# Issuing the loads of five meta weight groups one weight unit sooner in the sync engine's list

## What is computed

```python
h = jnp.concatenate([filler, meta, x], axis=1)
u = rms_norm_2(h, pre_mix_gain[l])
proj = u @ w_in[l]
qa, ka, va, qb, kb, vb, g = jnp.split(proj, SPLITS, axis=-1)
...
k_meta = k[:, META_PAD:BLOCK]
v_meta = v[:, META_PAD:BLOCK]
```

## Time and profile before

| | |
|---|---|
| median of 3 runs | 842.55 us |
| the profiled execution, its own time | 842.99 us |
| its span | 841.1 us |
| TensorE busy with matmuls | 804.5 us (96%) |
| VectorE busy | 498.6 us (59%) |
| ScalarE busy | 468.4 us (56%) |
| mean granted clock of TensorE | 0.989 |
| loads of meta_w: issue to landing, median | 8.4 us |

### The profile page before, as it was taken

How to read it: one execution, slowest core, us unless ns; L and a number is a source line. 1 busy time by engine, 2 the same in 40 slices (tenths; PEclk the granted TensorE clock), 3 DMA queues, 4 the chain that set the end, 5 groups by cost and what they waited for, 6 DMA issues and landing times.

```text
span 841.1 us, 12690 instructions
## 1 busy us (share of the span) xinstructions
PE 804.5 (96%) x4238; PEld 651.6 (77%) x4238; DVE 498.6 (59%) x731; ACT 468.4 (56%) x1004; POOL 137.4 (16%) x204
## 2 busy tenths in 40 slices
PE   7999999999999995979999999999999999999996
PEld 5877877886777884767778888878887888888884
DVE  5456565584665555656666667666686644555454
ACT  5677585575666464436665656454656533444352
POOL 2011021000342110343335354100000000000000
PEclk9999999999999998899999999999999999999999
DMA  8974552468764546343233444556675646465631
GB/s 241 275 186 141 145 170 101 151 201 253 223 201 132 203 130 198 102 133 91 61 87 102 115 132 134 165 159 219 230 237 179 206 126 198 152 198 189 211 128 51
DMA packets 147294, 137.78 MB, mean 164 GB/s; under 512 B 15024, under 2 KB 115648, under 8 KB 147232
## 3 DMA queue, kind: packets, MB, share of 16 engines
q1 hardware_dynamic: 145136, 129.89, 50.2%
q0 software_dynamic: 2096, 7.09, 3.0%
HBM read 135.90 MB, written 1.05 MB: 163 GB/s over the span
## 4 chain that ended last, share of the span: by engine, by line
PE 80%; DMA 4%; POOL 4%; ACT 4%; DVE 3%; issue 2%; SPq 1%; DVEq 0%; ACTq 0%; POOLq 0%
PE psum L1176 64%; PE psum L1154 6%; DMA meta_w<-in_w_in 4%; PE psum L1275 3%; PE psum L1410 3%; PE psum L1196 1%; ACT w_hi L1457 1%; POOL rtmp L1122 1%; PE psum L1378 1%; POOL rtmp L1124 1%; DVE w_lo L1653 1%; POOL rtmp L1126 1%; POOL stage L1128 1%; DMA raw<-in_w_in 1%; ACT probs L1584 1%
## 5 line engine op out<-in xcount | busy, mean ns | idle before, releaser
L1653 DVE TENSOR_TENSOR w_lo<-raw,w_hi 128x1024 fp32r<-128x1024 f32 (+1 forms) x234 | 273.9, 1193 | 121.6 <-ACT w_hi L1457 85.8
L1176 PE MATMUL psum<-w_hi,h_hi 128*128 128x512 f32 (+1 forms) x656 | 259.3, 395 | 5.0 <-DVE h_lo L1711 4.1
L1457 ACT ACTIVATE w_hi<-raw 128x1024 fp32r<-128x1024 f32 (+1 forms) x234 | 230.8, 1011 | 44.2 <-PE psum L1176 18.6
L1176 PE MATMUL psum<-w_lo,h_hi 128*128 128x512 f32 (+1 forms) x656 | 246.8, 376 | 0.0
L1176 PE MATMUL psum<-w_hi,h_lo 128*128 128x512 f32 (+1 forms) x656 | 246.3, 375 | 0.0
L1176 PEld LDWEIGHTS psum<-w_hi,h_hi 128*128 128x128 f32 x656 | 124.0, 189 | 31.6 <-issue 15.0
L1176 PEld LDWEIGHTS psum<-w_lo,h_hi 128*128 128x128 f32 x656 | 123.7, 189 | 19.2
L1176 PEld LDWEIGHTS psum<-w_hi,h_lo 128*128 128x128 f32 x656 | 124.1, 189 | 15.3
L1176 PE MATMUL psum<-w_hi,m_hi 128*128 128x512 f32 x152 | 60.3, 397 | 1.6 <-DVE m_lo L1711 1.5
L1176 PE MATMUL psum<-w_lo,m_hi 128*128 128x512 f32 x152 | 59.3, 390 | 0.0
L1176 PE MATMUL psum<-w_hi,m_lo 128*128 128x512 f32 x152 | 59.2, 389 | 0.0
(11 more groups left out here) (171 smaller groups left out, 1006.0 us busy)
## 6 DMA issues: line engine op xcount, KB each, us to landing
raw<-in_w_in SPq DMA_DIRECT2D x112, 256.0 KB, 3.6
raw<-in_w_ffn_in SPq DMA_DIRECT2D x88, 256.0 KB, 4.0
raw<-in_w_in SPq DMA_DIRECT2D x24, 512.0 KB, 3.9
raw<-in_w_out SPq DMA_DIRECT2D x24, 512.0 KB, 3.5
raw<-in_w_in SPq DMA_DIRECT2D x64, 192.0 KB, 2.7
raw<-in_w_ffn_out SPq DMA_DIRECT2D x22, 512.0 KB, 4.4
meta_w<-in_w_in SPq DMA_DIRECT2D x10, 1024.0 KB, 8.4
raw<-in_w_mem_kv SPq DMA_DIRECT2D x8, 512.0 KB, 3.6
```

Of the source, the lines that this page charges most:

```text
L1176: last = nc.tensor.matmul(psum[:, bank, 0:n], sx[name][:, c, t * P:(t + 1) * P], wx[:, kk, 0:n], start=u["first"] and kk == 0 and z == 0, ...
L1457: nc.scalar.activation(weights(u)[0][:, :, 0:n], raw[:, u["raw"], :, 0:n], ACT.Copy)\
L1653: nc.vector.tensor_tensor(lo[:, :, 0:n], raw[:, u["raw"], :, 0:n], hi[:, :, 0:n].bitcast(F32), ALU.subtract)\
```

## The change

```diff
--- before.py
+++ after.py
@@ -716,7 +716,8 @@
     units = [arg for what, arg in line if what in ("unit", "unit_a") or (what == "flush" and arg and "chunks" in arg)]
     for g in metas:
         at = line.index(("meta", g) if g["n"] != 3 else ("flush", dict(g=g)))
-        after = sum(any(arg is u for u in units) for what, arg in line[:at] if what != "unit_b")
+        after = sum(what in ("unit", "unit_a") or (what == "flush" and arg is not None and "chunks" in arg)
+                    for what, arg in line[:at])
         units[after + META_LOAD[g["n"]]]["then_meta"] = g
     pl.steps = lay_out(line)
     number(pl, pl.steps)
```

## The result

The changed kernel takes 834.39 us (median of 4 runs, 833.52 to 835.22); the kernel before, run beside it, 842.28 us (840.41 to 844.26). The ratio is 0.9906, with a 95% interval of 0.988 to 0.9932: faster by 0.9%, 7.9 us. The forecast was 835.2, with a range of 832.6 to 838.6.

What follows compares the result with a forecast made beforehand. TensorE, busy 804.5 of 841.1 us, bounds the kernel, so only its waits and clock can give. Terms 1.1 + 5.6 + 0.6 = 7.3 us, from 842.55 to 835.2 us; range 832.6 to 838.6.

Steps and rivals of the forecast that it cites:

- Groups 0 and 2: TensorE's waits for the meta weights ahead of these groups go: 0.9 and 0.2 us, together 1.1 us.
- The pair leaves at once after group 3's matmuls: Group 4's two load DMAs wait only for group 3's matmuls and leave at 322.05 us, 5.0 us sooner.
- Its landing: Group 4's pair takes 8.7 us and lands at 330.75 instead of 336.37 us, a gain of 5.6 us.
- The clock: At group 4 the clock still falls in the idle time, costing 1.7 instead of 2.3 us: 0.6 us back.
- The norm as the next bound: At full clock, normed tile 0 sets the start of the transposes behind group 4, allowing at most 7.4 us.
- (a): Rival: ring order alone, no traffic ahead of group 4's pair; load gain 6.9 us, total 8.6, 833.9 us; chance 0.24.
- (b): Rival: the clock doesn't fall in group 4's 3 us wait; gains 8.8 us, 833.8 us; chance 0.12.
- signs that the forecast is wrong: Pair over 10 us, growing `xn` or `h_lo` wait, 0.50 clock beyond 4.6 us, or new `w_hi` or `w_lo` waits.
- signs that it is right: `meta_w` wait about 3.0 us, pair leaving at once, landing 8 to 9 us later, no new `raw` wait, TensorE less busy.
- (c): Rival: the unit behind slows group 4's pair to 10.9 us; gains 5.1 us, 837.4 us; chance 0.09.
- (d): Rival: gain handed back by another wait, further clock falls or a load leaving no sooner; 841 us or so; chance 0.05.
- (e): Rival: moved units land late and hold ScalarE's split, 20 us lost less 7.3 won; 855 us; chance 0.03.

Runs made afterwards that it cites:

- groups 0 to 3 alone: Kernel before, with only the load pairs of groups 0 to 3 issued one unit sooner; 840.56 us, ratio 0.9984.
- two units sooner: Changed kernel, with group 4's pair of loads issued one more unit sooner; 834.71 us, ratio 0.9918.
- filled kernel before: Kernel before, with 18 extra TensorE matmuls, never read, in the wait ahead of group 4; 839.73 us, ratio 0.9969.
- norm ahead of splits: Changed kernel, with the splits of two weight units moved behind the first norm at the border of the blocks; 836.23 us, ratio 0.9933.
- group 4 alone: Kernel before, with only group 4's pair of loads issued one unit sooner; 833.3 and 834.89 us in two comparisons.
- waits filled: Changed kernel, with extra unread matmuls: four ahead of group 4's, one behind them, two behind tile 0's transposes; 832.67 and 833.12 us.

## Why the prediction was right

- **Groups 0 and 2: 1.1 us. Held.** Both waits are gone, groups 0 to 3 alone give 1.05 us, and the mean start of group 3's last matmuls is 1.07 us sooner. The split was off: group 0's wait is the whole of it, group 2's is there in two of six profiles. That they come on top of group 4's gain in the time was not shown: two comparisons gave -1.1 and +0.3 us.
- **The pair leaves at once after group 3's matmuls, 5.0 us sooner. Held.** It leaves 1.12 us after their start, before 6.12: 5.0 us. The run with two units sooner shows that nothing but `meta_done` sets it.
- **Its landing: mis-sized.** The term was 8.7 us, taken from group 1's pair, with 7.4 as the high end. It took 7.8, and 7.5 to 7.8 in the other profiles in which nothing is ahead of it. That made the wait 2.17 us instead of 3.0, and the gain at group 4's matmuls 6.5 us instead of 5.6. The row of group 1 had 512 KB just ahead, and I had this written down and didn't take it off.
- **The clock: right in sum, wrong in place.** I had it fall in the wait and cost 1.7 instead of 2.3 us. In the profiled execution the wait passed at 1.00, group 4's matmuls took 1.91 us, and the fall came in the first products and cost 1.5. In a second execution it fell at the end of the wait. The filled kernel before measured the clock's full price as 1.4 to 2.05 us (I had 2.1 to 2.3).
- **The norm as the next bound: named, but not counted in.** It was said to bind only if the clock holds, at 7.4 us for the transposes. It did: from group 3's last matmuls, the transposes start 7.27 us sooner, and the wait for `xn` is 0.86 us. This is what kept rivals (a) and (b) from adding up: the load of (a), 6.9 us, and the clock of (b), 2.1 us, make 9.0, and the border up to the first product shows 7.69. A growing wait for `xn` stood among the signs that the forecast is wrong, and this sign came true. Of the signs that it is right, a lower busy time of TensorE showed in the border only (0.6 us less) and not in the whole span (0.1 us less).
- **The sum: close, and in part by luck.** Forecast for the border 5.6 + 0.6 = 6.2 us, measured 6.16 in the first two profiles. Two errors stand against each other in this: the landing gave 0.9 more and the new wait for the norm took it back. The fall of the clock costs about what I had put down, in another place. The agreement to a tenth is luck, since two profiles of each kernel allow 5.5 to 7.1. So is part of the agreement of the whole: of the 7.9 us, 1.0 is the difference between two executions ahead of group 0.
- **Rivals.** The time doesn't decide between them: 834.39 us lies between the forecast's 835.2 and the 833.9 of (a), a little nearer to (a), and the interval of the ratio holds both and the 833.8 of (b). By the traces, (a) is nearest in its load and (b) in its clock, each up to the norm. (c), a pair slowed by the unit behind, fell: with a unit right behind (two units sooner) it took 7.6 us, with the next unit 8.4 us behind (norm ahead of splits) 7.5. (d) and (e) fell: the part behind the border differs by 0.4 us, and the waits of ScalarE for `raw` are 13.6 us for `w_in` in both profiles. A second fall of the clock behind the border, as in (d), did come in, but the kernel before has it in its second profile, too. (In the working of (e), 3 x 2.4 is 7.2 and not 7.3, which changes nothing.)

The Trainium skill (DMA: Bandwidth & Descriptors, Queues, rings and completion order), by which descriptors of one ring are consumed in ring order, agrees with the landings: from the first issue of the pair to its last landing, 7.5 to 7.8 us with no load on the way ahead, whatever comes behind; 9.1 to 10.1 with one unit ahead (kernel before twice, filled, and groups 0 to 3 alone); 9.9 with two. With two units sooner a unit comes right behind the pair and none is ahead, and it is 7.6 us: so what is ahead counts, and by how much one unit does varies by 1 us.

## What to carry to other kernels

Where an engine that runs a fixed list waits for a load, look for what releases the *issue* of that load: here the pair stood behind a unit that had to wait 3.6 us for its buffer, and passing that unit was worth 5 us, while one place more was worth nothing. Count off what stands ahead of a load in its queue, and not what stands behind it. And before adding gains up, find what is ready next: the norm cut the best case by 0.9 us, and behind it a wait's end can still move a fall of the clock into work that had been free of it.

## What I had not expected of the hardware

The granted clock fell to 0.50 (1.2 GHz) in the middle of back-to-back products, at about 333.2 us, after three waits of 2.17, 0.86 and 1.25 us that TensorE had each passed at 1.00. The same kernel had it at the end of the wait in another execution (border 17.87 us), and the kernel with group 4 alone once not at all (17.26) and once at the first product (18.81). With the waits filled it didn't fall there in either profile. So a fixed order of work with short gaps has borders of 17.3 to 18.8 us from execution to execution.

The falls behind the border vary as well. Between 353 and 381 us the kernel before has one (at 361) in its first profile and two (at 359 and 376) in its second, and group 4 alone has one in both; each is 3.4 us at half clock and so costs up to 1.7 us. The medians of group 4 alone in its two comparisons, 833.3 and 834.89 us, are 1.6 us apart; its two profiles, 3.0 us apart, have 1.55 of that in the border, 0.39 ahead of it and 1.06 behind.
